# Seven products for eight: mixer output, cross keys, values and queries of a two-layer decoder trunk on one core

## The reference

```python
merged = sigmoid(g_ssd) * (y_ssd @ w_ssd_o) + sigmoid(g_attn) * (y_attn @ w_attn_o)
h = h + merged @ w_out                    # mixer output: (256,1024) @ (1024,1024)
q = rms_norm(h) @ w_cq                    # cross queries
k, v = split(rms_norm(mem) @ w_ckv)       # cross keys and values, mem is (256,1024)
h = h + softmax(q k^T / 16) v @ w_co      # 4 heads
h = h + hier_moe(rms_norm(h))             # top group, then 2 of its 8 experts
```

## Time and profile before

| | |
|---|---|
| median of 3 runs | 1627.74 us |
| the profiled execution's own time | 1625.95 us |
| its span, first to last instruction | 1624.0 us |
| mean granted TensorE clock | 0.966 |
| PE busy | 1472.3 us, 91% |
| DVE / ACT / POOL busy | 513.5 / 341.1 / 66.1 us |
| HBM read | 347.5 MB, 215 GB/s over the span |

### The profile page before, as it was taken

One profiled execution on the slowest core, in us unless ns is written; L12 is line 12 of the kernel. 1 busy time (PEld: TensorE's weight loads), 2 busy tenths in 40 slices (PEclk: granted clock), 3 DMA queues, 4 the chain that ended last, 5 costly groups with the idle time before them and its releaser, 6 DMA issues.

```text
span 1624.0 us, 19661 instructions
## 1 busy us (share of the span) xinstructions
PE 1472.3 (91%) x7988; PEld 1002.0 (62%) x7988; DVE 513.5 (32%) x1232; ACT 341.1 (21%) x658; POOL 66.1 (4%) x62
## 2 busy tenths in 40 slices
PE   7999999999999997777699999999999999786784
PEld 5885658888567553244268855688886575443341
DVE  3473447401300341111135634563022013312122
ACT  2222547300001120001022224472000021210010
POOL 0000320000000000000000013100000000000000
PEclk9999999999999998899899999999999999989897
DMA  8344223236441569999963342223273415899996
GB/s 298 144 156 153 77 87 126 107 131 233 156 155 52 207 258 413 400 419 415 395 223 138 127 150 105 104 105 108 104 273 117 154 52 207 337 410 420 416 419 261
DMA packets 115673, 349.59 MB, mean 215 GB/s; under 512 B 11664, under 2 KB 13968, under 8 KB 99216
## 3 DMA queue, kind: packets, MB, share of 16 engines
...
...
HBM read 347.50 MB, written 1.05 MB: 215 GB/s over the span
## 4 chain that ended last, share of the span: by engine, by line
PE 75%; issue 15%; DMA 7%; DVE 2%; ACT 1%; DVEq 0%; SPq 0%; POOL 0%; POOLq 0%
PE bank L701 27%; PE bank L682 23%; PE bank L879 7%; DMA ga<-in_w_down_e 4%; PE bank L658 3%; PE bank L1022 3%; PE bank L993 2%; DMA wring<-in_w_up_e 2%; PE bank L817 2%; PE bank L1058 1%; PE bank L918 1%; PE bank L806 1%; PE bank L842 1%; PE bank L862 1%; PE bank L1041 1%
## 5 line engine op out<-in xcount | busy, mean ns | idle before, releaser
L701 PE MATMUL bank<-hT,wring 128*128 128x256 f32 x1536 | 337.6, 380 | 1.2 <-issue 1.2
L701 PEld LDWEIGHTS bank<-hT,wring 128*128 128x128 f32 x1536 | 289.7, 190 | 43.9 <-issue 4.9
L682 PE MATMUL bank<-wring,hT 128*128 128x512 f32 (+2 forms) x576 | 217.5, 535 | 0.0
L1022 PE MATMUL bank<-wring,big 128*32 128x256 f32 x2048 | 142.9, 441 | 60.1 <-DMA wring<-in_w_up_e 43.3
L682 PEld LDWEIGHTS bank<-wring,hT 128*128 128x128 f32 x576 | 104.8, 192 | 105.1 <-issue 103.3
L1022 PEld LDWEIGHTS bank<-wring,big 128*32 128x32 f32 x2048 | 71.5, 126 | 129.5 <-DMA wring<-in_w_up_e 47.2
L879 PE MATMUL bank<-big,wring 128*128 128x256 f32 x512 | 111.0, 379 | 2.0 <-ACT big L1143 2.0
L879 PEld LDWEIGHTS bank<-big,wring 128*128 128x128 f32 x512 | 97.1, 190 | 15.6 <-issue 2.5
L993 PE MATMUL bank<-big,xn 128*128 128x256 f32 x256 | 76.7, 463 | 21.5 <-DVE big L1659 20.4
L993 PEld LDWEIGHTS bank<-big,xn 128*128 128x128 f32 x256 | 68.2, 335 | 32.4 <-DVE big L1659 25.4
L1386 DVE SCALAR_TENSOR_TENSOR scr<-bank,prm,scr 128x255 f32<-128x255 f32 (+1 forms) x144 | 62.7, 477 | 58.3 <-ACT scr L1111 55.6
...
## 6 DMA issues: line engine op xcount, KB each, us to landing
wring<-in_w_in SPq DMA_DIRECT2D x68, 1024.0 KB, 7.0
...
wring<-in_w_ssd_o SPq DMA_DIRECT2D x16, 1024.0 KB, 6.3
...
wring<-in_w_ckv SPq DMA_DIRECT2D x16, 1024.0 KB, 7.4
...
ga<-in_w_down_e SPq DMA_DIRECT2D x8, 2048.0 KB, 30.6
```

Source lines behind the costliest of these rows:

```text
L682: ins = nc.tensor.matmul(bank[bank_of(job)][:, 0:width], src[:, k, t * P:(t + 1) * P], wring[:, SLOT[c], k, 0:width], start=i == 0, stop=i ...
L701: ins = nc.tensor.matmul(bank[bank_of(job)][:, i * SEQ:(i + 1) * SEQ], wring[:, SLOT[c], k, m:m + P], src[:, k, :], start=n == 0, stop=n = ...
L1022: ins = nc.tensor.matmul(bank[b][j * S:(j + 1) * S, i * F:(i + 1) * F], xg[:, k, e:e + S], up_part[i][:, j, k * F:(k + 1) * F], start=k == ...
```

## The change

Each of the eight stages a layer splits input (256 tokens by 1024) and weight chunk (1024 by 512) into two by two blocks and forms the product with seven block products instead of eight (the Winograd form of Strassen's scheme). A block product is 128 tokens by 512 by 256 columns, one job each, in the order 1, 2, 5, 6, 3, 7, 4. Products 1 and 2 use blocks as they are; the others use sums of input blocks, sums of weight blocks, or both.

* DVE makes the four input sums, once per input (`merged`, `mem`, `h`): 128x512 each, in a new stage `sums`.
* GpSimd makes four weight sums for each chunk, 128x1024 elements each: two in a scratch area (`wsum1`, `wsum2`) and two in place in the ring slot. The first of a stage waits for the chunk and for product 5 of the stage before.
* ACT copies products 1 and 5 out of PSUM; DVE does all the rest (`combine`).
* The scratch takes the fourth slot of the ring, so the ring has three slots. Chunk c now waits for chunk c-3. The gate weights of the first expert pass wait for the last job of `("co", 0)`, instead of that of `("cq", 1)`.

```diff
-    o += [("ssdo", 0), ("ssdo", 1), ("atto", 0), ("atto", 1), ("wo", 0), ("wo", 1)]
-    o += [("memT", i) for i in range(4)] + [("ck", 0), ("ck", 1), ("cv", 0), ("cv", 1)]
-    o += [("norm", 1)] + [("hT", 1, i) for i in range(4)] + [("cq", 0), ("cq", 1)]
+    o += [("ssdo", 0), ("ssdo", 1), ("atto", 0), ("atto", 1), ("sums", "merged"), ("wo", 0), ("wo", 1)]
+    o += [("memT", i) for i in range(4)] + [("sums", "mem"), ("ck", 0), ("ck", 1), ("cv", 0), ("cv", 1)]
+    o += [("norm", 1)] + [("hT", 1, i) for i in range(4)] + [("sums", "h"), ("cq", 0), ("cq", 1)]
...
+SEVEN = {"wo": "merged", "ck": "mem", "cv": "mem", "cq": "h"}
+PRODUCTS = (1, 2, 5, 6, 3, 7, 4)
+UNITS = [st for st in ORDER if st[0] in SEVEN]
+INPUTS = [st[1] for st in ORDER if st[0] == "sums"]
+
+
 def make_jobs():
     jobs = []
     for st in ORDER:
-        if st[0] == "part":
+        if st[0] in SEVEN:
+
+            jobs += [(st, p, "act" if p in (1, 5) else "dve") for p in PRODUCTS]
...
-W_SLOTS = 4
+W_SLOTS = 3
+HALF_W = NCOL // 2
...
-        wring = sb("wring", [P, W_SLOTS, KC, NCOL])
+        wring = sb("wring", [P, W_SLOTS + 1, KC, NCOL])
...
+        spare_slot = wring[:, W_SLOTS, :, :].rearrange("p k n -> p (k n)")
+        wsum1 = cols(spare_slot, 0, KC // 2, HALF_W)
+        wsum2 = cols(spare_slot, 1024, KC // 2, HALF_W)
+        prod1, prod5, part2, part3, part4, whole = [cols(spare_slot, 2048 + i * HALF_W, HALF_W) for i in range(6)]
+        sums_of = {"merged": cols(qq[:, 0, :], 0, 4, KC // 2, P), "mem": cols(big, 4096, 4, KC // 2, P),
+                   "h": xn[:, :, :].rearrange("p t (s k n) -> p (t s) k n", s=2, n=P)}
+        source_of = {"merged": mgT, "mem": memT, "h": hT}
...
-                        filled(sp, l, last_job(NCH - W_SLOTS + 2 * i + 1))
+                        filled(sp, l, last_job(NCH - 2 + i))
...
+            def weight_sums(l, st, which):
+
+                u = UNITS.index(st)
+                c = CHUNK[(st, 0)]
+                w = wring[:, SLOT[c], :, :]
+                k = KC // 2
+                w11, w12 = w[:, 0:k, 0:HALF_W], w[:, 0:k, HALF_W:NCOL]
+                w21, w22 = w[:, k:KC, 0:HALF_W], w[:, k:KC, HALF_W:NCOL]
+                at = (l * len(UNITS) + u) * 4
+                for n in which:
+                    if n == 1:
+                        pool.wait_ge(w_in_sem[SLOT[c]], landed(l, c))
+                        if u:
+                            filled(pool, l, JOB[(UNITS[u - 1], 5)])
+                        out, a, b = wsum1, w12, w11
+                    elif n == 2:
+                        pool.wait_ge(wsum_rdy, at + 1)
+                        if u:
+                            filled(pool, l, JOB[(UNITS[u - 1], 6)])
+                        out, a, b = wsum2, w22, wsum1
+                    elif n == 3:
+                        out, a, b = w12, w22, w12
+                    else:
+                        pool.wait_ge(wsum_rdy, at + 3)
+                        filled(pool, l, JOB[(st, 2)])
+                        out, a, b = w21, wsum2, w21
+                    nc.gpsimd.tensor_tensor(out, a, b, ALU.subtract).then_inc(wsum_rdy, 1)
...
-                for k in (3, 4):
-                    power(l * NORMS + k, st_[:, 18:20])
+                power(l * NORMS + 3, st_[:, 18:20])
+                for st in UNITS:
+                    weight_sums(l, st, (1, 2, 3))
+                    if st == ("cq", 0):
+                        power(l * NORMS + 4, st_[:, 18:20])
+                    weight_sums(l, st, (4,))
...
+                for p in PRODUCTS:
+                    x, w, ws, xn_ = {1: (x11, w11, 0, 0), 2: (x12, w21, 0, 0), 3: (xs_[:, 3], w22, 0, 3),
+                                     4: (x22, w21, 4, 0), 5: (xs_[:, 0], wsum1, 1, 1), 6: (xs_[:, 1], wsum2, 2, 2),
+                                     7: (xs_[:, 2], w12, 3, 4)}[p]
+                    job = JOB[(st, p)]
+                    free(l, job, made.get(p, []))
+                    if ws:
+                        pe.wait_ge(wsum_rdy, wat + ws)
+                    if xn_:
+                        pe.wait_ge(xsum_rdy, xat + xn_)
+                    b = bank[bank_of(job)]
+                    for i in range(2 if by_channel else 1):
+                        for j in range(k):
+                            if by_channel:
+                                ins = nc.tensor.matmul(b[:, i * P:(i + 1) * P], w[:, j, i * P:(i + 1) * P], x[:, j, :],
+                                                       start=j == 0, stop=j == k - 1)
+                            else:
+                                ins = nc.tensor.matmul(b[:, 0:HALF_W], x[:, j, :], w[:, j, :], start=j == 0, stop=j == k - 1)
...
-                    by_token(l, st, mgT, blocks_by={k: JOB[(("atto", k // 4), k % 4 // 2)] for k in range(KC)})
+                    made = {1: [JOB[(("atto", 0), j)] for j in range(2)], 2: [JOB[(("atto", 1), j)] for j in range(2)]}
+                    seven(l, st, made if st[1] == 0 else {})
...
+                elif kind in ("ck", "cq"):
+                    made = {"ck": [("memT", i) for i in range(4)], "cq": [("hT", 1, i) for i in range(4)]}[kind]
+                    seven(l, st, {1: [JOB[(m, 0)] for m in made]} if st[1] == 0 else {}, by_channel=True)
                 elif kind == "cv":
-                    by_token(l, st, memT)
-                elif kind == "cq":
-                    by_channel(l, st, hT, made_by=("hT", 1))
+                    seven(l, st, {})
...
+                elif kind in SEVEN:
+                    u = UNITS.index(st)
+                    for p, to, read in ((1, prod1, 6), (5, prod5, 4)):
+                        filled(act, l, JOB[(st, p)])
+                        if u:
+                            drained(act, l, JOB[(UNITS[u - 1], read)])
+                        drain_inc(nc.scalar.activation(to, bank[bank_of(JOB[(st, p)])][:, 0:HALF_W], ACT.Copy), JOB[(st, p)])
...
+                job, b = product(2)
+                drained(dve, l, JOB[(st, 1)])
+                drain_inc(put(0, 0, b, prod1, ALU.add), job)
+                job, b = product(6)
+                drain_inc(V.tensor_tensor(part2, b, prod1, ALU.add), job)
+                drained(dve, l, job)
+                drained(dve, l, JOB[(st, 5)])
+                link(V.tensor_tensor(part4, part2, prod5, ALU.add))
+                job, b = product(3)
+                drain_inc(put(0, 1, b, part4, ALU.add), job)
+                job, b = product(7)
+                drain_inc(V.tensor_tensor(part3, b, part2, ALU.add), job)
+                drained(dve, l, job)
+                put(1, 1, part3, prod5, ALU.add)
+                job, b = product(4)
+                drain_inc(put(1, 0, part3, b, ALU.subtract), job)
...
+                    V.tensor_tensor(to[:, 0], x21, x22, ALU.add).then_inc(xsum_rdy, 1)
+                    dve.wait_ge(xsum_rdy, at + 1)
+                    V.tensor_tensor(to[:, 1], to[:, 0], x11, ALU.subtract).then_inc(xsum_rdy, 1)
+                    dve.wait_ge(xsum_rdy, at + 2)
+                    V.tensor_tensor(to[:, 3], x12, to[:, 1], ALU.subtract).then_inc(xsum_rdy, 1)
+                    V.tensor_tensor(to[:, 2], x11, x21, ALU.subtract).then_inc(xsum_rdy, 1)
...
+                        link(V.tensor_tensor(whole, x, y, op))
+                        link(V.tensor_tensor(hh, hh, whole, ALU.add))
+                        return dve.nop()
+
+                    combine(l, st, put)
+                    drained(dve, l, JOB[(st, 4)])```

The order of instructions on PE, layer 0, the two `ssdo` stages and the first matmuls of `atto` and `wo`. Before:

```order
L879 MATMUL bank<-big,wring 128x256 [waits drained_by_dve,drained_by_act,chunk_in1,chunk_in0]
L879 MATMUL bank<-big,wring 128x256 x31
L879 MATMUL bank<-big,wring 128x256 [waits drained_by_act,drained_by_dve]
L879 MATMUL bank<-big,wring 128x256 x31
L879 MATMUL bank<-big,wring 128x256 [waits drained_by_dve,chunk_in3,chunk_in2]
```

More of the change, by code:

```diff
@@ L146 @@
     "yT": (1, "both"), "ssdo": (2, "dve"), "atto": (2, "dve"),
-    "wo": (2, "dve"), "memT": (1, "both"), "ck": (2, "act"), "cv": (2, "act"), "cq": (2, "act"),
+    "memT": (1, "both"),
     "xscore": (1, "act"), "xprobT": (1, "act"), "xpv": (1, "dve"), "co": (2, "dve"),
@@ L447, in all_drained, with landed @@
                     drained(eng, l, max(mine))
+        def landed(l, c):
+            return (l * SLOT.count(SLOT[c]) + (NTH[c] + 1)) * 32
         def settle(eng):
@@ L665, in chunk_in @@
             def chunk_in(l, c):
[L666 removed]
+                pe.wait_ge(w_in_sem[SLOT[c]], landed(l, c))
             def by_token(l, st, src, width=NCOL, blocks_by=None, tile_by=None, tiles=range(TT), ks=range(KC)):
@@ L1305, in scale, with combine, product @@
                 return ins
+            def combine(l, st, put):
+                def product(p):
+                    job = JOB[(st, p)]
+                    filled(dve, l, job)
+                    return job, bank[bank_of(job)][:, 0:HALF_W]
+                job, b = product(2)
```

(37 more changed lines are left out.)

51 lines of the change are left out of this document (27 added, 24 removed).

## The result

The changed kernel takes 1674.28 us, the median of 4 runs (1673.87 to 1675.88), against 1627.54 us before (4 runs). The ratio is 1.0293, with a 95% interval of 1.0281 to 1.0305: 46.7 us slower, where 30.6 were forecast. The profiled execution takes 1673.99 us with a span of 1672.0, and a mean granted clock of 0.953 (0.966 before). PE's busy time is 1465.6 us (1472.3 before), GpSimd's 220.6 (66.1), DVE's 641.2 (513.5).

A forecast was written before the change was run, and what follows sets the result against it. PE, busy 91% of the span, was taken as the bound. Lost 27.2 us a layer, won 11.9: net +15.3, both layers +30.6 on 1625.95 gives 1656.6, plus 1.8 for the median: 1658 us, range 1642 to 1680 (8 in 10).

The forecast's parts named there:

- the forecast as summed: Whole kernel: PE's savings against its stops and slow clock give 1658 us; chance 72%.
- rival 1: Eight changed stages: every weight sum runs at the hindered rate, so GpSimd outlasts PE; 19 us a layer, 1696 us; chance 8%.
- What PE saves: Changed stages: seven products for eight save 3.2 us per wo or cv pair, 2.7 per ck or cq pair.
- the four stops: PE idle ahead of second ssdo (about 8 us), inside first wo (7), ahead of ck (2.4), ahead of hT (3 to 4).
- The semaphore waits of the products: Ahead of each product: taken as free; at 0.05 us for each of 112 products, 5 us, put into the range.
- A: Second ssdo stage: three slots make its load late; PE stops 7.9 us, plus clock 2.2: 10.1 us a layer.
- B: First wo stage: product 5 waits for a late first weight sum; 6.9 us stop plus clock 2.2: 9.1 us.
- D: Ahead of hT and cq: norm 1 now follows cv's last product; 3.4 us stop, 0.5 wait, clock 2.2: 6.1 us.
- C: memT to ck: more DVE operations end wo; idle grows from 1.63 to 2.4 us, plus 1.1 clock: 1.9 us.
- The clock: After PE stops of 3 us or more: granted clock falls to 0.50, charged at 2.2 us a stop.
- Rival 2: Behind the stops: the clock stays up or falls later, so the slow-clock charges go; 1643 us; chance 10%.
- Covered: No PE stop expected from weight sums (8.3 us a stage against 12.1 to 12.5), combine, other ring loads or gate weights.

The follow-up runs named there:

- r8: Changed kernel with ssdo taking first row halves first, norm 3 earlier, norm 1 between ck stages, wo products added straight from PSUM, squares on ACT: 1604.76 us.
- r1: Kernel before the change with only the ring of three slots and the later wait of the first pass's gate weights: 1647.03 us, ratio 1.0124.
- r3: Changed kernel with the ssdo stages doing the first half of the rows for all output blocks before waiting for the second half: 1653.79 us.
- r5: Changed kernel with norm 3 (of mem) made before the last gating of atto instead of after the input sums: 1655.09 us.
- r4: Changed kernel with norm 1 put before the ck stages instead of ahead of the hT transposes: 1666.3 us.
- r2: Changed kernel with each GpSimd weight sum replaced by an operation on 8 columns of a constant, all waits kept: 1653.77 us.
- r7: Kernel before the change plus 11 unused GpSimd subtractions of 128x1024 a layer, behind norm 3 beside the wo stages: 1633.51 us.

## Why the prediction came out right, and where it was off

The direction was right, and 1674.3 lies in the range of 1642 to 1680, near its upper end, 16 us above 1658. That it lies in it is in part luck: the forecast as summed had a range of its own of 1648 to 1670, which the measurement missed, and the room above 1670 was kept for a slow GpSimd (rival 1), which did not stop PE in `ck`, `cv` or `cq`. By its own steps:

* **What PE saves**, 11.9 us a layer. Right. The stages that run at full clock show it: `cv` 24.3 us, `cq` 25.3 us a pair, with 24.2 and 25.0 forecast. r8, in which three of the four stops are gone and the one ahead of `ck` is no longer than before the change, is 21.8 us faster than the kernel before, close to the 23.8. The semaphore waits of the products cost nothing that can be seen.
* **A**, 10.1 us a layer. Right, and shown twice: r1 adds it alone (20.4 us for both layers), r3 takes it out (20.5).
* **B**, 9.1 us a layer. Right as a stop (6.52 us for 6.9) and by the whole of `wo` (+5.6 for +5.9). r5 takes it out. Inside it two errors met. A weight sum takes 2.36 us, not 2.1: L625's second input is a broadcast, and these have two full inputs; that this is the reason wasn't tried. And the 0.6 us by which DVE's scaling was to hold up the first sum did not come: PE goes on 2.43 us after that sum begins, and it is the scaling that is held up (5.59 us for 1.42).
* **D**, 6.1 us a layer. Right in size (6.3) and place (4.12 us of idle for 3.4); r4 takes the stop out, with 4.0 us a layer over the whole kernel and 5.3 from `cv` to `cq` in layer 0. The step's own terms add up to 3.3, not 3.4. Part of the agreement is chance: with the weight sums left out (r2) the idle is 3.0 us, so that the 4.12 hold about 1.1 us of a wait that the step did not have.
* **C**, 1.9 us a layer, is the term that was mis-sized. It measured 7.4 from `memT` to `ck`, and `ck` itself ran 27.3 us for 25.0: 9.7 us. The difference of 7.8 us, twice, is 15.6 of the 16.3 us missing. The count of DVE's operations was right, as r2 shows (2.62 us of idle for 2.4). Wrong was the duration of each that reads two SBUF inputs, 0.42 us for the additions and 0.69 for the squares, carried over from a stretch without GpSimd; with weight sums beside them they took 1.9 to 2.5 and 2.6 to 2.7 us in the first `wo` stage of layer 0.
* **The clock.** 2.2 us a stop fits as a mean: `ck` loses 2.2 behind 6.45 us, `ssdo` 1.5 in layer 0 and 2.4 in layer 1. It is no fixed price: r1 loses 3.0 behind 8.59 us, in r2 the `ck` pair loses 1.7 us after 2.62 us of idle, and in r7 it loses 1.7 in layer 0 and nothing in layer 1, behind 3.75 and 3.76 us. Rival 2 is out.
* **Covered**: the gate weights and GpSimd's pace in `ck`, `cv` and `cq` were. `combine` in `wo` was not: 15 us for 4.6.

Rival 1 named the right collision and read one side of it. It took L633's 2.02 against 1.04 us beside L1468 as GpSimd being slowed, which is so, and asked only what a slow GpSimd would do. In that row L1468 too takes 1.98 us; with GpSimd at rest, at 163.42, it takes 1.22, and its mean over the kernel is 1712 ns. The rival also had GpSimd slowed by 3 to 4 us in each `wo` stage; its eleven sums there take 28.3 us for 26.0 at 2.36, and DVE pays. This row was the hint not followed:

```profile
163.42 1.22 DVE L1468 TENSOR_TENSOR scr<-scr,qiT 128x1024 f32<-128x1024 f32 x1 [1.18 <-ACT scr L1187]
...
170.85 1.04 POOL L631 TENSOR_TENSOR ga<-ga,tail 128x512 f32<-128x512 f32 x1 [8.10 <-PE bank L825]
...
L1468 DVE TENSOR_TENSOR scr<-scr,qiT 128x1024 f32<-128x1024 f32 x16 | 27.4, 1712 | 18.9 <-ACT scr L1187 18.9
```

L1468, begun at 171.00, ends at 172.98, 1.1 us behind the end of L631; L633, begun at 171.85, ends at 173.87, 0.9 us behind the end of L1468. So each is held up by the other's running operation, and what an engine pays depends on how long that operation is. There it was about 1 us on either side. Beside weight sums of 2.36 us, DVE's operations of 0.42 to 0.71 us pay up to 2.2 us each and GpSimd's up to 0.4.

The Trainium skill's sentence ("Advanced Engine Details and Errata", GPSIMD Details) speaks of a conflict on a shared interface and does not itself say who waits. The runs agree with it in that the DVE operations held up are those with two SBUF inputs and the scaling at 0.71 us for 1024 columns, where one with two inputs takes 1.22.
